# The first stage of a diffusion transformer step is reordered: wide modulation matmuls, sums of squares and second-order filter pairs moved in between the first order's spectra

## The reference

```
h = _rmsnorm(x, norm1_g) * (1.0 + scale1) + shift1
proj = h @ w_in                        # q, k, v, u_hy, gates
# Hyena filters, for L = 1024 and L = 256, two orders, 512 channels
emb = concat([t, cos(f * wpos), -sin(f * wpos)])        # L x 33
h = sin(fr * (emb @ w1 + b1)); h = sin(fr * (h @ w2 + b2))
h = (h @ w3).reshape(L, 2, HYENA_ORDER, D_HYENA) * decay
two_sided = [fwd[0] + bwd[0], fwd[1:], 0, reversed(bwd[1:])]
hf = rfft(two_sided)
```

## Time and profile before

| what | us |
|---|---|
| median of 3 runs (2787.21 to 2791.22) | 2788.02 |
| the profiled execution's own time | 2791.18 |
| its span, first to last instruction | 2789.3 |
| first matmul of the first stage's latent units | 89.69 |
| transpose of the reciprocal roots | 164.45 |
| first matmul of the second order's units | 169.76 |
| first matmul of the next stage | 225.63 |

### The profile page before, as it was taken

One profiled execution on the slowest core, in us unless ns is written; L12 is line 12 of the kernel. 1 busy time (PEld: TensorE's weight loads), 2 busy tenths in 40 slices (PEclk: granted clock), 3 DMA queues, 4 the chain that ended last, 5 costly groups with the idle time before them and its releaser, 6 DMA issues. The chain is left out here.

```text
span 2789.3 us, 36190 instructions
## 1 busy us (share of the span) xinstructions
PE 2686.1 (96%) x14803; PEld 2312.8 (83%) x14803; DVE 1273.1 (46%) x1853; ACT 896.0 (32%) x1512; POOL 827.7 (30%) x552
## 2 busy tenths in 40 slices
PE   9788999989999999999999799999999999999998
PEld 7567888878888888898887688887888888888887
DVE  6667765545655454445677611435221211212216
ACT  2343221045555455545311521224112121121122
POOL 3546995211001010100244133314233233232230
PEclk9779999999999999999999899999999999999999
DMA  6666776442122312320669422301111111111102
GB/s 205 224 204 233 245 238 212 155 159 97 67 86 92 112 59 96 109 82 34 234 218 324 147 91 87 129 30 42 41 40 38 38 38 38 38 38 38 39 31 76
DMA packets 99027, 314.27 MB, mean 113 GB/s; under 512 B 12065, under 2 KB 29571, under 8 KB 98478
## 3 DMA queue, kind: packets, MB, share of 16 engines
q1 hardware_dynamic: 75726, 231.73, 24.3%
q0 software_dynamic: 23136, 80.22, 8.6%
HBM read 232.75 MB, written 70.78 MB: 109 GB/s over the span
## 5 line engine op out<-in xcount | busy, mean ns | idle before, releaser
L2490 DVE SCALAR_TENSOR_TENSOR tl_x<-tl_b,all_mod,tl_x 128x512 f32<-128x512 f32 (+1 forms) x216 | 142.7, 662 | 351.2 <-PE tl_b L91 348.2
L89 PE MATMUL at_out<-h_hi,hd_nexthi 128*128 128x424 f32 (+1 forms) x672 | 264.6, 394 | 6.7 <-PEq L77 3.4
L89 PE MATMUL tl_b<-tl_hi,tl_whi 128*128 128x512 f32 (+1 forms) x720 | 255.9, 355 | 1.2 <-ACT tl_r L2325 1.2
L90 PE MATMUL tl_b<-tl_lo,tl_whi 128*128 128x512 f32 (+1 forms) x720 | 255.4, 355 | 0.0
L91 PE MATMUL tl_b<-tl_hi,tl_wlo 128*128 128x512 f32 (+1 forms) x720 | 255.0, 354 | 0.0
L540 POOL TENSOR_TENSOR hd_nextlo<-at_raw,hd_nexthi 128x1024 fp32r<-128x1024 f32 x26 | 61.4, 2360 | 628.9 <-ACT hd_nexthi L640 628.9
L722 DVE TENSOR_REDUCE at_nmax<-at_s 128x1 f32<-128x1280 f32 (+1 forms) x160 | 196.9, 1273 | 105.0 <-PE at_s L591 104.3
L90 PE MATMUL at_out<-h_lo,hd_nexthi 128*128 128x424 f32 (+1 forms) x672 | 239.8, 357 | 0.0
L91 PE MATMUL at_out<-h_hi,hd_nextlo 128*128 128x424 f32 (+1 forms) x672 | 239.7, 357 | 0.0
L675 ACT ACTIVATE at_e<-at_s,at_nmax 128x1280 f32<-128x1280 f32 (+1 forms) x160 | 185.3, 1159 | 135.8 <-DVE at_nmax L722 135.8
L2580 DVE TENSOR_TENSOR tl_r<-tl_r 128x512 f32<-128x512 f32 (+1 forms) x96 | 65.7, 686 | 356.3 <-ACT tl_r L2325 356.3
(11 more groups left out here) (340 smaller groups left out, 6383.0 us busy)
## 6 DMA issues: line engine op xcount, KB each, us to landing
hy_tab<-in_hy_tab POOLq DMA_DIRECT2D x68, 512.0 KB, 5.5
mg_nextraw<-in_w_tail SPq DMA_DIRECT2D x36, 512.0 KB, 3.7
tl_raw<-in_w_tail SPq DMA_DIRECT2D x36, 512.0 KB, 3.6
hd_wa<-in_w_adaT SPq DMA_DIRECT2D x32, 512.0 KB, 4.4
at_raw<-in_w_proj SPq DMA_DIRECT2D x26, 512.0 KB, 4.6
fd_in<-in_xT SPq DMA_DIRECT2D x16, 640.0 KB, 4.5
s_gatesT<-at_pad SPq DMA_DIRECT2D x16, 640.0 KB, 2.9
mg_gate<-s_gatesT SPq DMA_DIRECT2D x16, 640.0 KB, 5.0
```

Of the source, the lines that this page charges most:

```text
L89: pe.matmul(out, w_hi, x_hi, start=first, stop=False)
L90: pe.matmul(out, w_hi, x_lo, start=False, stop=False)
L2490: dve.scalar_tensor_tensor(out=x1[:, n, at:at + m], in0=bank[x % GEMM_BANKS][:, 0:m], scalar=g.mod[:, gate, SEG_OF[c]:SEG_OF[c] + 1], in1= ...
```

## The change

- The modulation weights are laid out in 8 blocks of 256 output columns, each in two halves of the contraction. The conditioning vectors are now the weights (two columns) and the block is the moving operand; ScalarE copies the two resulting rows to SBUF (`ada_out`) and TensorE turns them back by two products with the identity (`ada_turned`).
- The first of six steps of a sine argument moves from VectorE to ScalarE (`pre`). The two sums of the last layer's weights and their low part move to GpSimd. The wide blocks 0 to 2 stand ahead of the three layer 2 products.
- All 8 rows of x are squared and summed by matmuls while the first order's pairs and context units are made; `sum_up` is gone. The rows of x pass behind the modulation blocks (`stream_items`).
- The first order's context units stand between its pairs. The second order's five pairs stand between the first order's latent units (`PAIR_ORDER`). They go to four homes instead of two buffers.
- Odd units come ahead of even units. The second order's context and odd slots are split during the first order's units, its even slots during the second order's context units. GpSimd makes all low parts of filter slots; before, VectorE made ten of them.
- Five `ob` buffers instead of four; all stores are issued by SP, none by GpSimd.
- Each row of x has a place of its own for `h`, in the low part's room, and is loaded by SP in the last four units of the first order, after all pairs are made.
- The decay table is loaded in two parts. The stage has 82 semaphores instead of 69 (the next stage has 30). In the next stage four buffers change places.

```diff
-    return ctx + [(LAT_FT, 2), (1, 2)] + [(j, c) for j in low for c in range(2)]
+    odd, even = ([j for j in low if even_tile(j) == e] for e in (False, True))
+    return (ctx + [(LAT_FT, 2)] + [(j, c) for j in odd for c in range(2)] + [(1, 2)]
+            + [(j, c) for j in even for c in range(2)])
...
+PAIR_ORDER = [(0, 0), (0, 1), (0, 2), (0, 3), (0, 4), (1, 1), (1, 0), (1, 2), (1, 3), (1, 4)]
+PAIR_HOME = [1, 0, 1, 0, 1, 0, 2, 3, 1, 2]
...
             for i in range(STREAM + 3, len(ITEMS)):
+                load(i)
+            for x in range(2 * R):
...
+                for dst, src in stores(x):
+                    sp.dma_start(dst, src).then_inc(stored[x % OB], 16)
+                if x < R and x + 1 in ROWS_AFTER:
+                    sp.wait_ge(made, len(PAIR_ORDER))
+                    for k in range(2 * ROWS_AFTER.index(x + 1), 2 * ROWS_AFTER.index(x + 1) + 2):
+                        sp.dma_start(x_row[k][:], g.d["xT"][k]).then_inc(row_in[k], 16)
...
         @block.tensor
-                    for k in range(KD):
-                        mm = pe.matmul(pm[:, n, :], w[:, k], g.silu[:, k], start=(k == 0), stop=(k == KD - 1))
+            def ada(b):
+                if b:
+                    pe.wait_ge(ada_row, b)
+                for q in range(2):
+                    i = 2 * b + q
+                    pe.wait_ge(*landed(ADA_AT[i]))
+                    w = stream[ADA_AT[i] % STREAM][:, 0:D].rearrange("p (k c) -> p k c", k=ADA_K)
+                    for k in range(ADA_K):
+                        mm = pe.matmul(p_ada, g.silu[:, ADA_K * q + k], w[:, k], start=(q == 0 and k == 0),
+                                       stop=(q == 1 and k == ADA_K - 1))
                     mm.then_inc(ada_mm, 1)
+            def ada_turned(b):
+                pe.wait_ge(ada_row, b + 1)
+                for j in range(ADA_N // P):
+                    mm = pe.matmul(pm[:, ADA_N // P * b + j], row_buf[:, j * P:(j + 1) * P], g.ident[0:2, 0:2], ...)
...
+            for i in range(NET):
+                ada(i)
+                layer(1, i)
+                ada_turned(i)
+            ada(3)
+            taps_of(0)
+            ada_turned(3)
+            token_sum(0)
+            ada(4)
+            taps_of(1)
+            unit(0)
+            unit(1)
+            ada_turned(4)
+            token_sum(1)
+            ada(5)
+            taps_of(2)
+            unit(2)
+            unit(3)
...
+            taps_of(5)
+            token_sum(6)
+            token_sum(7)
+            for u, s in ((CTX_UNITS, None), (CTX_UNITS + 1, 6), (CTX_UNITS + 2, 7), (CTX_UNITS + 3, None), (ODD_UNITS, 8),
+                         (ODD_UNITS + 1, None), (ODD_UNITS + 2, 9), (ODD_UNITS + 3, None)):
+                if s is not None:
+                    taps_of(s)
+                unit(u)
+            pe.wait_ge(rstd_done, 1)
+            pe.transpose(p_rows, rstd[:], g.ident[:]).then_inc(rows_mm, 1)
+            unit(ODD_UNITS + 4)
...
+            mm.then_inc(spread, 1)
+            for u in range(M):
+                unit(M + u)
...
         @block.vector
+            for s in range(1, 6):
+                pair(s)
+            cross(CTX_UNITS)
+            pair(6)
+            cross(CTX_UNITS + 1)
+            pair(7)
+            cross(CTX_UNITS + 2)
+            cross(CTX_UNITS + 3)
+            pair(8)
+            cross(ODD_UNITS + 1)
...
+            pair(9)
+            cross(ODD_UNITS + 2)
...
+            multiply(0)
+            multiply(1)
+            for i in range(4):
+                cross(M + CTX_UNITS + i)
+                multiply(2 + i)
+            cross(M + ODD_UNITS + 1)
+            multiply(6)
+            lower(0)
```

More of the change, by code:

```diff
@@ L908, in stage_head @@
[L908 to L913, removed]
@@ L995, in stores @@
             return [(sp_[partner(j) if part == "odd" else j, :, c, :], out[:])]
-        def sent(x):
-            return (stored if x < BY_SP else stored_late)[x % OB]
         def stored_by(x):
[L1002 to L1012, removed]
+            return stored[x % OB], 16 * sum(len(stores(y)) for y in range(x % OB, x + 1, OB))
         def landed(i):
@@ new lines, in ada_turned, with token_sum @@
+            def ada_turned(b):
+                pe.wait_ge(ada_row, b + 1)
+                for j in range(ADA_N // P):
+                    mm = pe.matmul(pm[:, ADA_N // P * b + j], row_buf[:, j * P:(j + 1) * P], g.ident[0:2, 0:2], start=True,
+                                   stop=True)
+                mm.then_inc(ada_turn, 1)
+            def token_sum(k):
+                pe.wait_ge(squared, k + 1)
+                x = stream[X_AT[k] % STREAM]
+                for tt in range(TT):
+                    mm = pe.matmul(p_sum[:, k, tt:tt + 1], x[:, tt * P:(tt + 1) * P], g.ones[:, 0:1], start=True, stop=True)
+                mm.then_inc(token_sums, 1)
@@ new lines, in _ @@
+            pe.wait_ge(rstd_done, 1)
+            pe.transpose(p_rows, rstd[:], g.ident[:]).then_inc(rows_mm, 1)
+            unit(ODD_UNITS + 4)
+            pe.wait_ge(rows_done, 1)
+            pe.wait_ge(late_in, 16 * 7)
+            pe.wait_ge(mixed, len(PAIR_ORDER))
+            for c, (at, m) in enumerate(CHUNKS):
+                for tt in range(at // P, (at + m) // P):
+                    mm = pe.matmul(spread_bank[c][:, tt * P - at:tt * P - at + P], pick[:, tt], rows[:], start=True,
+                                   stop=True)
@@ new lines, in _ @@
+            pre(0, 0)
+            pre(0, 1)
+            sine(0, 0)
+            pre(0, 2)
+            act.wait_ge(w3_sum, 2)
+            act.activation(w3_hi[:], w3[:], ACT.Copy).then_inc(w3_h, 1)
+            sine(0, 1)
+            pre(1, 0)
+            ada_out(0)
+            sine(0, 2)
+            pre(1, 1)
+            sine(1, 0)
+            net_out(0)
+            ada_out(1)
+            pre(1, 2)
+            sine(1, 1)
+            net_out(1)
+            sine(1, 2)
+            net_out(2)
@@ new lines, in _ @@
+            ada_out(2)
+            ada_out(3)
+            square(0)
+            act.wait_ge(late_in, 16 * 7)
+            first_split(0)
+            ada_out(4)
+            square(1)
+            scale(0)
+            scale(1)
+            first_split(1)
+            ada_out(5)
+            square(2)
+            scale(2)
+            scale(3)
+            first_split(2)
+            ada_out(6)
+            square(3)
+            scale(4)
+            first_split(3)
+            ada_out(7)
@@ new lines, in _ @@
+            square(4)
+            square(5)
+            first_split(4)
+            square(6)
+            square(7)
+            scale_unit(CTX_UNITS)
+            scale_unit(CTX_UNITS + 1)
+            act.wait_ge(made, PAIR_ORDER.index((1, 0)) + 1)
+            for i in range(CTX_AT, ODD_AT):
+                upper(i)
+            scale_unit(CTX_UNITS + 2)
+            scale_unit(CTX_UNITS + 3)
+            scale_unit(ODD_UNITS)
+            act.wait_ge(spec_mm, ODD_DONE)
+            odd_split(1)
@@ L1479, in _ @@
+            dve.wait_ge(std_done, 1)
+            dve.reciprocal(rstd[:], std[:]).then_inc(rstd_done, 1)
+            cross(ODD_UNITS + 3)
+            dve.wait_ge(rows_mm, 1)
+            dve.tensor_copy(rows[:], p_rows).then_inc(rows_done, 1)
+            cross(ODD_UNITS + 4)
             dve.wait_ge(a_done, 1)
```

652 lines of the change are left out of this document (327 added, 325 removed).

## The result

| | before | after |
|---|---|---|
| time, median of the runs, us | 2787.64 (2787.21 to 2791.22) | 2814.86 (2814.67 to 2818.02) |
| ratio to before, 95% interval | | 1.0097 [1.0084, 1.0109] |
| profiled span, us | 2789.3 | 2816.1 |
| first matmul of the next stage, us | 225.63 | 252.02 |
| from there to the end of the span | 2563.7 | 2564.1 |

What follows compares the result with a forecast made beforehand. TensorE, busy 96% of the span, was taken to bound the kernel. The next stage starting at 200 instead of 225.6 saves 25.6, less 1.3 for semaphores: 24.3 us, giving 2763.7 us (8 in 10: 2744 to 2782).

Steps and rivals of the forecast that it cites:

- Five `ob` buffers and all stores on SP: Second order's units, first stage: removes the waits for stores (ScalarE's 37.3 us before), leaving VectorE late next.
- Wide modulation form: First stage's modulation matmuls: 3.7 us a block fast, 4.1 with its turn against 3.88; can only change the clock.
- Network, +6.9: Sine network at the first stage's start: first taps at 39.7 us against 32.77 before.
- TensorE waiting over 5 us in all for the turns' row copies: First stage, TensorE: listed as a sign that the prediction is wrong; size over 5 us in all.
- First latent unit at 105: First order: from first taps at 39.7, 65.2 us (54.2 TensorE work, 5 last split, 6 slow stretches); 89.7 before.
- the 6 us for slow stretches: First taps to first latent unit: 6 us added because TensorE runs partly at 1.2 GHz around sums and turns.
- Latent units and pairs, 41 us, spread 3.5: First order's latent units with second order's pairs between: VectorE 41 us, to 146; then spread 3.5, to 149.5.
- Second order's units, 50.5 us from the spread to 200: First stage's end: first latent unit at 161.2, last crossing 196.7, next stage at 200 instead of 225.63.
- Semaphores, +1.3: Later stages: one clear moves to the heads' end and a second comes at the very end, +1.3 us.
- C: Rival, first stage: port contention slows VectorE sums (+6.3) and products and low parts (+9.3, 6 already in); 2773 us; chance 0.14.
- D: Rival: TensorE at 1.2 GHz from first taps, first latent unit at 155, decided from 129.3; 2814 us; chance 0.06.
- SP's stores coming late enough to stop `ob`: First stage, SP waiting for pair 9: a sign of being wrong; ScalarE and TensorE would stand up to 7 us.

Runs made afterwards that it cites:

- e1: The changed kernel with SP's six stores of 127 partitions each cut into 112 and 15 partitions: 2771.64 us.
- e6: The changed kernel with SP's six stores of 127 partitions each cut into 113 and 14 partitions: 2809.79 us.
- e5: The changed kernel with SP's six stores of 127 partitions each cut into 121 and 6 partitions: 2775.49 us.
- e2: The kernel before, with the six stores of 127 partitions issued whole by ScalarE instead of GpSimd, semaphore limit 104: 2852.27 us.
- e3: As e2, the kernel before with these stores issued by ScalarE, but each cut into 112 and 15 partitions: 2796.83 us.
- e8: e1 with the modulation products in the old narrow form (128 weight columns, 2 moving), without row copies and turns: 2788.48 us.
- e11: e1 run once more unchanged, as the base for runs beside it: 2775.58 us.
- e9: e1 with modulation block 2's rows copied earlier, the first taps ahead of its turn and block 3, and a semaphore limit of 120: 2767.88 us.
- e7: e1 with SP issuing the eight x rows one at a time and later, instead of two at a time: 2776.28 us.

## Why the prediction was wrong, step by step

**The step that failed** is in the second order's units: "Five `ob` buffers and all stores on SP (2.2 us to land against 5.9 from GpSimd) take the stores' waits away, and VectorE is late next." The row it rests on was right and was read too far. The 2.2 us are those of six stores of 256 KB, 128 partitions; GpSimd's 5.9 are the median of 32 stores of 256 KB. Neither says anything of the 254 KB stores, which before had been issued by GpSimd only. In their place the runs showed some 10 us for each on SP and waits of 57.3 and 42.3 us. The step's price is 43.2 us (the kernel after minus e1), with 34.3 from e6 minus e5 and 55.4 from e2 minus e3. The pair "127 partitions, SP" was treated as shown though no row of before has it; it should have been bounded from both sides and carried as a rival. The rule of the Trainium skill told at e6 would have named it.

The other steps:

- *Wide modulation form.* Its fast price was right: 3.7 forecast, 3.62 measured. "It can only change the clock" was right and named no amount. The amount is 16.8 us by e8 minus e1 (12.9 by e8 minus e11), as much as e1's whole gain over before (16.7): e8, without it, is no faster than before.
- *Network, +6.9.* Measured +11.5 in the kernel after, +9.4 in e1, +10.8 in e11. The walk charged the turns' row copy as a hand-over of 0.6 to 0.7; it stood behind the sine and cost TensorE 5.29 us at 37.02, of 9.2 in three such waits. The prediction had listed "TensorE waiting over 5 us in all for the turns' row copies" as a sign that it is wrong, and that sign came true. e9 brings the three waits down to 3.7 us, and puts the taps ahead of block 3.
- *First latent unit at 105.* 107.3, 101.1 and 107.3 in three profiles (after, e1, e11): right within their spread, and in part by luck. From the first taps on 65.2 us were forecast and 63.0, 58.9 and 63.8 measured. The work, 54.2 at full clock, was close (52.2, 52.2 and 51.7 by busy time times clock). But the 5 us for the last split didn't show: TensorE waited at most 1.5 us in all. And the 6 us for slow stretches were 9.2, 5.8 and 12.1. The two errors cancel.
- *Latent units and pairs, 41 us, spread 3.5.* In e1 the first latent unit to the end of the spread is 48.3 us, against 44.5 forecast. In the kernel after it is 50.6, without a wait for stores until 146.8.
- *Second order's units, 50.5 us from the spread to 200.* In the kernel after 94.2. In e1 55.2 (149.4 to 204.6), and the 4.7 us too much lie ahead of VectorE's first crossing of a latent unit, not behind it: it was forecast at 161.2 and came at 168.53, after a wait of 12.3 us for a store, while the DMA engines were full (404 GB/s). From there on VectorE took 36 us where 39 were forecast. The waits for stores that should be near zero are 28.8 us even in e1.
- *Semaphores, +1.3.* The two clears stand where they were put. Their price is not shown: from the next stage's first matmul to the end it is 2564.1 us against 2563.7 before, and 2558.7 to 2564.1 over the kernels made from the changed one:

```profile
L82 POOLq EVENT_SEMAPHORE_RANGE_CLEAR  x2: 637/646/654, 586.9 to 2815.2; - x2
```

Of the rivals, C's slowdown is in the traces, and nearer to the size of the forecast. In e1 three products of x and one low part on VectorE take 6.9 us more than at 1.67 each, where the sum had +6 and C +9.3. Each of the four starts while GpSimd makes a low part and ends 1.1 to 1.5 us behind it. Products and low parts that start beside none take 1.67, even where the DMA engines are full:

```profile
175.67 1.67 DVE L1559 SCALAR_TENSOR_TENSOR fd_xrow<-fd_xrow,fd_a,fd_acc 128x256 f32<-128x256 f32 x2
178.61 3.46 DVE L1559 SCALAR_TENSOR_TENSOR fd_xrow<-fd_xrow,fd_a,fd_acc 128x256 f32<-128x256 f32 x2
...
177.62 2.96 POOL L1155 TENSOR_TENSOR h_lo<-fd_xrow,h_hi 128x1280 fp32r<-128x1280 f32 x1 [0.80 <-PE fd_b L91]
...
175.67:177.34 1.67, 0.53 (x1) 1.00 1.02 324
186.44:188.10 1.66, 0.68 (x1) 1.00 0.83 262
195.22:199.74 4.52, 3.43 (x2) 0.50 0.30 116
```

The last three rows are windows with GpSimd's busy time, TensorE's granted clock, DMA share and GB/s. A product of 1.67 us stands at a DMA share of 1.02 and a low part of 1.67 us at 0.83, the low part of 4.52 us at 0.30. So the transfers are not what slows these.

D's 2814 is the measured time within a microsecond and D is wrong: it wanted latent units at 155 behind a TensorE at 1.2 GHz, decided from 129.3, and they came at 107.25, with 48.72's block at full speed. A time that agrees proves no mechanism; the station does. "SP's stores coming late enough to stop `ob`" was the other sign that came true. It had been given no chance, and a price of at most 7 us, for SP's wait for pair 9 alone.

**Still open.** e1's 2771.6 and e11's 2775.6 lie 8 and 12 us above 2763.7. By stations, e1's profile is 2.5 us late in the network, 6.3 early up to the first latent unit, 3.8 late in the latent units and the spread, and 4.7 late behind it, 4.6 in all; e11's is 3.8 late, 1.4 early, 2.1 late and 7.1 late, 11.5 in all. Another part is the step from the profiled execution to the median: the forecast took off 3.2 us, but e1's profiled execution, at 2767.5, was 4.2 us under its median and within 1 us of the 2766.9 forecast for it. That agreement is luck too: the next stage began 4.6 us late, and the rest of the program took 4.1 us less than was charged. Open are why e3 stays 8.5 us above the kernel before, why the clock granted to one kernel differs between executions, and why e7 gains nothing.

## What to carry over

Before a transfer changes its issuer, look up its partition count and which issuer's row in the profile has that same shape: a landing time is a property of shape and issuer together, and a median over a group of another shape says nothing of it. On SP's and ScalarE's queues, cut a partition count such as 127 so that a large divisor is left (112 and 15, or 121 and 6, but not 113 and 14). A busy stretch of TensorE isn't at full clock merely because it is busy: in e8 it had 0.74. The wide form saved no instruction time here and still was worth 13 to 17 us, so such a change is priced by the clock of its stretch and not by its instructions.

## What the runs showed of the hardware

- While a store of 127 partitions from SP was in flight alone, the rate was 23 to 27 GB/s and 6.6% of the sixteen engines' time was used; 254 KB take some 10 us at that, an estimate. With 113 partitions the rate was 20 to 27 (e6), and with 127 from ScalarE 21 to 27 (e2). 112 partitions landed in 3.9 us, 128 in 3.9, and 127 from GpSimd in 3.4.
- Two pairs of x rows on SP took 10.81 and 15.13 us to issue in the kernel after, at 145.67 and 157.96; in e1 no pair took over 1.64. That the slow store ahead held them up is argued, not shown: in e6, with stores as slow, no pair took over 2.64, while three stores behind one pair spread over 13.86.
- Eight fp32 products of 256 moving columns are 16 instructions in the trace and took 3.62 us at 2.4 GHz (granted clock 1.00 at 48.72). With such products in place of narrow ones the clock of the stretch from 44 to 70 us is 0.93 instead of 0.74, at equal busy time, worth 13 to 17 us here. The Trainium skill, TensorE: Matmul & The Clock Gate, section "Loop structure matters more than you think", has dense work keep the clock up. The trace of e8 disagrees: its stretch from 44 to 70 us was busy for all 26.00 us, narrow products among the rest, and had 0.74.
- A product or low part on VectorE over one row block of x took 1.67 us, and 2.58 to 4.52 when it started while GpSimd made a low part (e1).
